# A four-head matrix-memory mixer: the attention moved into the o projection, memories handled in strips of 32, new states a projection later, stores from ScalarE's queue

## The reference

```python
w_inter = jnp.exp(inter - m_t)
s = jnp.einsum('bhtk,bhsk->bhts', q, k) * jnp.exp(d - m_t[..., None])
num = w_inter[..., None] * jnp.einsum('bhtk,bhkv->bhtv', q, C) + jnp.einsum('bhts,bhsv->bhtv', s, v)
den = w_inter * jnp.einsum('bhtk,bhk->bht', q, n) + jnp.sum(s, axis=-1)
h = num / jnp.maximum(jnp.abs(den), jnp.exp(-m_t))[..., None]
...
wk = w_k[..., None] * k
C_new = decay_prev[..., None, None] * C + jnp.einsum('bhsk,bhsv->bhkv', wk, v)
n_new = decay_prev[..., None] * n + jnp.sum(wk, axis=2)
```

## Time and profile before

| | |
|---|---|
| three runs | 2731.1 us median (2729.4 to 2731.57) |
| the profiled execution | span 2730.8 us from first to last instruction |
| TensorE, its weight loads | 2631.1 us (96%), 2523.8 us (92%) |
| VectorE, ScalarE, GpSimd | 1405.0 us (51%), 1004.8 us (37%), 222.7 us (8%) |
| heads | first projection from 47.28 us, the first gated layer from 713.77 us |
| mean granted clock of TensorE | 0.985 |
| HBM | 363.40 MB read, 23.43 MB written |

### The profile page before, as it was taken

One profiled execution on the slowest core, in us unless ns is written; L12 is line 12 of the kernel. 1 busy time (PEld: TensorE's weight loads), 2 busy tenths in 40 slices (PEclk: granted clock), 3 DMA queues, 4 the chain that ended last, 5 costly groups with the idle time before them and its releaser, 6 DMA issues. The chain is left out here.

```text
span 2730.8 us, 44822 instructions
## 1 busy us (share of the span) xinstructions
PE 2631.1 (96%) x16761; PEld 2523.8 (92%) x16761; DVE 1405.0 (51%) x2094; ACT 1004.8 (37%) x1345; POOL 222.7 (8%) x306
## 2 busy tenths in 40 slices
PE   7999999999999999999999997599999999999998
PEld 5969789797999999999999997599999999999997
DVE  5444444444754454454445446965455454554545
ACT  4323333233443332333333336244343342333435
POOL 1110201102200000000000003610000000000002
PEclk9999999999999999999999998799999999999999
DMA  4545445454344444444444434144444444444443
GB/s 137 163 153 164 164 124 166 156 163 162 125 143 149 144 140 141 140 140 133 151 144 133 147 128 134 48 142 149 153 144 151 149 147 149 146 149 148 141 141 108
DMA packets 224748, 389.77 MB, mean 143 GB/s; under 512 B 25829, under 2 KB 53045, under 8 KB 223965
## 3 DMA queue, kind: packets, MB, share of 16 engines
q1 hardware_dynamic: 222511, 382.93, 44.0%
q10 hardware_dynamic: 2045, 4.00, 0.4%
HBM read 363.40 MB, written 23.43 MB: 142 GB/s over the span
## 5 line engine op out<-in xcount | busy, mean ns | idle before, releaser
L1019 DVE TENSOR_TENSOR w_lo<-w_raw,w_hi 128x1024 fp32r<-128x1024 f32 x664 | 815.9, 1235 | 1043.8 <-ACT w_hi L759 1041.5
L759 ACT ACTIVATE w_hi<-w_raw 128x1024 fp32r<-128x1024 f32 x664 | 699.0, 1058 | 1364.6 <-PE bank L419 1328.8
L417 PE MATMUL bank<-xh,w_hi 128*128 128x336 f32 (+2 forms) x3584 | 1135.6, 317 | 49.6 <-issue 23.2
L418 PE MATMUL bank<-xl,w_hi 128*128 128x336 f32 (+2 forms) x3584 | 1129.7, 315 | 0.0
L419 PE MATMUL bank<-xh,w_lo 128*128 128x336 f32 (+2 forms) x3584 | 1127.4, 315 | 0.0
L417 PEld LDWEIGHTS bank<-xh,w_hi 128*128 128x128 f32 x3584 | 676.7, 189 | 58.5 <-issue 44.9
L419 PEld LDWEIGHTS bank<-xh,w_lo 128*128 128x128 f32 x3584 | 678.5, 189 | 0.0
L418 PEld LDWEIGHTS bank<-xl,w_hi 128*128 128x128 f32 x3584 | 677.7, 189 | 0.3
L417 PE MATMUL bank<-hh,w_hi 128*128 128x336 f32 (+1 forms) x1632 | 511.7, 314 | 4.5 <-issue 4.5
L419 PE MATMUL bank<-hh,w_lo 128*128 128x336 f32 (+1 forms) x1632 | 511.4, 313 | 0.0
L418 PE MATMUL bank<-hl,w_hi 128*128 128x336 f32 (+1 forms) x1632 | 511.3, 313 | 0.0
(11 more groups left out here) (247 smaller groups left out, 1257.4 us busy)
## 6 DMA issues: line engine op xcount, KB each, us to landing
w_raw<-in_w_up SPq DMA_DIRECT2D x640, 256.0 KB, 2.8
w_raw<-in_w_down SPq DMA_DIRECT2D x336, 256.0 KB, 3.4
w_raw<-in_w_mlstm_in SPq DMA_DIRECT2D x192, 256.0 KB, 3.1
area<-in_state_mlstm_C SPq DMA_DIRECT2D x32, 512.0 KB, 5.3
w_raw<-in_w_mlstm_out SPq DMA_DIRECT2D x64, 256.0 KB, 3.0
out_C_sample<-area SPq DMA_DIRECT2D x32, 512.0 KB, 3.0
w_raw<-in_w_up SPq DMA_DIRECT2D x64, 192.0 KB, 2.5
w_raw<-in_w_pool SPq DMA_DIRECT2D x16, 256.0 KB, 3.1
```

Source lines behind the costliest of these rows:

```text
L417: pe.matmul(out, wh, xhk, start=first, stop=False)
L418: pe.matmul(out, wh, xlk, start=False, stop=False)
L759: nc.scalar.activation(w_hi[:, s], w_raw[:, s], ACT.Copy).then_inc(hi_done, 1)
L1019: V.tensor_tensor(w_lo[:, s], w_raw[:, s], w_hi[:, s].bitcast(F32), ALU.subtract).then_inc(lo_done, 1)
```

## The change

What a head computes stays the same. The 64 sample tokens are padded: 8 sequences stand as 4 strips of 32 columns, each with 16 columns of padding and two sequences. All eight memories have a buffer, some of them in places that other tiles of the head use at another time; memory 0 shares its place with q and k.

- The o projection uses banks SA, so SB is free beside it. The transposed values stand before chunk 17, denominators and own numerators before chunk 19, past numerators before chunk 20, the transposes of the normalised heads before chunk 23. The prompt states stand behind chunk 23 and wait for banks of o that have been read out.
- Past numerators: 16 matmuls with 32 stationary columns, each group of four to four strips of one bank. New states: one fp32 matmul a memory and half of the keys, with 32 contracted rows (one strip holds two sequences; the weights of the other one are zero), in four rounds of four strips to four banks. These rounds, and VectorE's updates, stand in the q and k projection of the next head, and after the last head in the first projection of the first feed-forward. Stabilisers move from chunk 5 to chunk 7 in heads 1 to 3.
- Stores of new memories leave SP's queue for ScalarE's, four behind the high part of chunk 8 and four behind that of chunk 10. Loads of memories stand on SP before chunks 14, 16 and 18.
- Sums of squares and roots take places in the shared area in place of tiles of their own; GpSimd clears what is padded, and the split of keys and values for the new states is gone.

```diff
+TA = 3 * 128
+STRIPS, PER = 4, 2
...
+            def c_loads(h, batch):
+                for b in batch:
+                    if b == 0:
+                        wait_apart(sp, sp_passed, kt_ready, h + 1)
+                        wait_apart(sp, sp_passed, qm_ready, h + 1)
+                    elif not isinstance(h, int):
+                        sp.wait_ge(c_stored[b], 16 * h)
...
+                        if (blk, k) == (0, 6):
+                            if isinstance(h, int):
+                                sp.wait_ge(gcol_mm, 1)
+                            c_loads(h, (2, 4, 6))
+                        if (blk, k) == (1, 0):
+                            c_loads(h, (1, 3, 5, 7))
+                        if (blk, k) == (1, 2):
+                            c_loads(h, (0,))
...
-                    sp.wait_ge(c_updated, NB * h + b + 1)
-                    sp.dma_start(dst[b].rearrange("h (k p) v -> p (h k) v", p=P)[:, bass.ds(2 * h, 2), :],
-                                 Cr[:, b % 4]).then_inc(c_stored[b % 4], 16)
...
+            def new_states(h, e):
+
+                def products(r):
+                    i, k = r // 2, r % 2
+                    if r == 0:
+                        pe.wait_ge(evac, e)
+                        pe.wait_ge(wkb_ready, h + 1)
+                    else:
+                        pe.wait_ge(c_updated, 16 * h + 4 * r)
+                    for s in range(STRIPS):
+                        own = slice(32 * s, 32 * s + 32)
+                        pe.matmul(SB[s][:, :], wkb[own, i, k * P:(k + 1) * P], vtok[own, 2, :],
+                                  start=True, stop=True).then_inc(cnew_ready, 1)
+
+                return {at: (lambda r=r: products(r)) for r, at in enumerate((1, 2, 4, 5))}
...
+                def past_numerators():
+
+                    for b in range(NB):
+                        pe.wait_ge(c_landed[b], 16 * (h + 1))
+                    for i in range(PER):
+                        for k in range(2):
+                            for s in range(STRIPS):
+                                b = PER * s + i
+                                pe.matmul(SB[2][32 * s:32 * s + 32, :], qm[:, k, b, :], Cr[b][:, k, :],
+                                          start=False, stop=False, skip_group_check=True)
+                    pe.matmul(SB[2][:, :], PS2, vtok[:, 2, :], start=False, stop=True).then_inc(num_ready, 1)
...
-                gemm(SB, c, 16, KT, 4, xh, xl, 0, free=after(e + 4), amid={3: values})
...
-                    for k in range(2):
-                        new, ks = SB[2 * (b % 2) + k][:, :], slice(k * P, (k + 1) * P)
-                        pe.matmul(new, wkbh[0:TL, b % 2, ks], vh[0:TL, :], start=True, stop=False)
-                        pe.matmul(new, wkbh[0:TL, b % 2, ks], vl[0:TL, :], start=False, stop=False)
-                        m_ = pe.matmul(new, wkbl[0:TL, b % 2, ks], vh[0:TL, :], start=False, stop=True)
-                    m_.then_inc(cnew_ready, 1)
...
+                gemm(SA, c, 16, KT, 4, xh, xl, 0,
+                     guard={0: (ps_ready, h + 1), 1: (ktok_ready, h + 1)},
+                     amid={1: values, 3: own_numerators, 4: past_numerators, 7: hidden})
...
+                    pe.wait_ge(evac, e + (8 + (1, 4)[k]))
+                    for s in range(3):
+                        m_ = pe.matmul(SA[2 + k][:, :], wkp[:, s, k * P:(k + 1) * P], vtok[:, s, :],
                                        start=(s == 0), stop=(s == 2))
...
+            def c_stores(h, i):
+                for b in range(i, NB, PER):
+                    act.wait_ge(c_updated, 16 * h + 8 * (i + 1))
+                    act.dma_start(O["C_sample"][0][b].rearrange("h (k p) v -> p (h k) v", p=P)[:, bass.ds(2 * h, 2), :],
+                                 Cr[b]).then_inc(c_stored[b], 16)
...
                 his(c, 4, 9)
+                if not first:
+                    c_stores(h - 1, 0)
+                    his(c, 9, 11)
+                    c_stores(h - 1, 1)
...
+                if not first:
+                    dve.wait_ge(c_stored[0], 16 * h)
...
-                new_states(0, NB - 1)
...
+            def update(h, c, k0):
+
+                for r in range(4):
+                    i, k = r // 2, r % 2
+                    for s in range(STRIPS):
+                        b = PER * s + i
+                        dve.wait_ge(cnew_ready, 16 * h + (4 * r + s + 1))
+                        V.scalar_tensor_tensor(Cr[b][:, k], Cr[b][:, k], WI[:, NS * b + NS - 1:NS * b + NS],
+                                               SB[s][:, :], ALU.mult, ALU.add).then_inc(c_updated, 1)
+                    los(c, k0 + (4, 5, 7, 8)[r], k0 + (5, 7, 8, 9)[r])
...
+                    if first and q == 0 and i == 0:
+                        update(H - 1, c, k0)
+                        dve.wait_ge(c_stored[0], 16 * H)
+                        V.memset(E[:, :, 0:2], 0.0).then_inc(e_zero, 1)
+                        los(c, k0 + 9, k0 + 11)
...
+                for i in range(PER):
+                    m_ = G.tensor_scalar(wkb[:, i], ktok[:, 2], wsum[:, 4 + i:5 + i], None, ALU.mult)
+                m_.then_inc(wkb_ready, 1)
```

More of the change, by code:

```diff
@@ L181, in program, with owned @@
+        qn = view(15270, 2 * P).rearrange("p (k n) -> p k n", k=2)
+        Cr = [view(at, 2 * DV).rearrange("p (k n) -> p k n", k=2)
+              for at in [0] + [8614 + i * 2 * DV for i in range(6)] + [15526]]
+        def owned(ap, n=32):
+            return ap.rearrange("p (s c) -> p s c", c=n)[:, :, n - 16:]
         xtok = view(0, 3 * D).rearrange("p (s n) -> p s n", n=D)
@@ L184, in program @@
         ntok = view(6784, DK, NB * H)
[L185 to L188, removed]
+        wgr = view(8614, KT * 8).rearrange("p (k n) -> p k n", n=8)
+        wgg = view(8742, KT * 36).rearrange("p (k n) -> p k n", n=36)
+        sqr = view(9318, 4 * T).rearrange("p (s n) -> p s n", n=T)
+        row = [view(10662 + i * T, T, 36) for i in range(12)]
+        rpad = [view(7528 + i * P, P, H) for i in range(2)]
         E = view(0, 4 * GW).rearrange("p (f t) -> p f t", t=GW)
@@ L483, in sum_squares @@
                 pe.wait_ge(ssq_ready, k)
-                pe.matmul(out, ones[:, :], acc[:, :], start=True, stop=True).then_inc(rms_mm, 1)
+                pe.matmul(out, ones[:, :], sums[k], start=True, stop=True).then_inc(rms_mm, 1)
+            def new_states(h, e):
[11 more added lines that the diff above has]
+                return {at: (lambda r=r: products(r)) for r, at in enumerate((1, 2, 4, 5))}
             def head(h, c, e):
@@ new lines, in hidden @@
+                def hidden():
+                    pe.wait_ge(n_read, h + 1)
+                    pe.wait_ge(hn_ready, 3 * h + 3)
+                    for s, (t0, n) in enumerate(((0, P), (P, P), (2 * P, P))):
+                        for f in range(4):
+                            m_ = pe.transpose(SB[f][:, t0:t0 + n], hn[:, s, f * P:(f + 1) * P], ident[:, :])
+                    m_.then_inc(ht_ready, 1)
+                gemm(SB, c, 8, KT, 4, xh, xl, 0, free=None if first else after(e - 4), guard=guard, amid={2: scores})
@@ L597, in head @@
-                pe.wait_ge(den_read, h + 1)
-                for k in range(2):
-                    out = SA[3][:, 16 * k:16 * k + 1 + NB]
-                    pe.matmul(out, ktok[0:TL, 2, k * P:(k + 1) * P], X[0:TL, X2 + META - 1:XW:NS], start=True, stop=False)
-                    pe.matmul(out[:, 0:1], ktok[:, 0, k * P:(k + 1) * P], X[:, X1 - 1:X1], start=False, stop=False)
-                    m_ = pe.matmul(out[:, 0:1], ktok[:, 1, k * P:(k + 1) * P], X[:, X2 - 1:X2], start=False, stop=True)
@@ L1433, in _ @@
             sum_of_squares(1)
[L1435 to L1436 removed]
+            for b in range(NB):
+                pool.wait_ge(c_stored[b], H * 16)
             pool.wait_ge(cst_stored, 16 * H)
```

454 lines of the change are left out of this document (226 added, 228 removed).

## The result

The changed kernel takes 2658.0 us (median of four runs, 2656.3 to 2658.8) against 2731.2: 0.9731 of the time before, 95% interval 0.9717 to 0.9745. That is 73.2 us less. Predicted were 33 us less (2698); the measured time lies near the lower end of the stated range and beside the rival of four strips abreast (2654).

What follows compares the result with a forecast made beforehand. TensorE, busy 2631.1 of 2730.8 us, was taken as the bound. A head gains 27.5 + 0.6 − 17.8 − 1.4 − 0.2 − 0.7 = 8.0 us; four heads 32, with the start 33: 2698 us, own range 2685 to 2712, whole range up to 2734.

Steps and rivals of the forecast that it cites:

- four strips abreast: Rival for past numerators and new states: all four strips run together, 6.9 us a head, 2654 us; chance 0.14.
- The strips: Past numerators and new states: 32 strip matmuls at one pass each, with group ends and weight loads 17.8 us a head.
- loads of weights: New states: loading weights 128 columns wide shows once strips share the array, 16 × 0.11 = 1.8 us a head.
- The bound below: Lower bound for strip matmuls: four abreast, eight groups at 0.86 us, 6.9 us a head.
- One after another: Rival: strips do not overlap, 27.5 us a head; 2737 us, or 2749 if strip changes cost too; chance 0.17.
- a late queue: Rival: a store or wait on ScalarE, SP or VectorE holds something back four times; 2718 us, chance 0.11.
- The loop: Attention's loop over the eight memories, up to the prompt state, goes: 27.5 us a head gained.
- the prompt state waits: End of the o projection: new wait until a bank of o is read out, 0.7 us a head.
- the steps into and out of a round: Seven more pieces inside projections each cost 0.2 us beyond their work, 1.4 us a head.
- the start: Kernel start: VectorE no longer waits 2.24 us for GpSimd's clearing ahead of the gates; 1 us taken as gain.
- The forecast's own lower end: Lower end of the forecast's own range, 2685 us: loads of weights hidden, 1.8 us a head.
- What was costed at nothing: Updates, squares, normaliser and scaling beside projections, and the stores' and loads' queues: delays covered, no cost taken.

Runs made afterwards that it cites:

- The run with one strip: Changed kernel without the past numerators of strips 1 to 3 (12 of 16 matmuls a head left out): 2676.5 us, ratio 0.9800.
- the two orders: Changed kernel with past numerators reordered: four matmuls in a row on each strip, 2680.1 us; two in a row on each strip, 2659.0 us.
- the full rows: Changed kernel with new states contracting all 128 rows instead of a strip of 32: 2692.8 us, ratio 0.9857.
- the run on SyncE's queue: Changed kernel with the stores of updated memories put back from ScalarE's queue to SyncE's: 2657.3 us, ratio 0.9730.
- The mends: Changed kernel, first gated layer's rounds a chunk later: 2656.4 us; rounds before chunks 2, 4, 5, 6 and third bank of o read earlier: 2651.0 us.

## Why the prediction was wrong

The direction and what bounds the kernel were right; the size was off by 40.0 us (2698 − 2658.0), and one step of the sum failed.

*The strips.* The step was that "the next strip's first pass starts no earlier than that second pass", so that a strip matmul costs 0.43 us: 17.8 us a head. The first passes of four strips start together, and their second passes too. The steps measured are 3.57 + 4 × 1.07 = 7.85 us a head; 9.95 less, over four heads 39.8 of the 40.0. The run with one strip shows that the other three cost nothing, the two orders show how far ahead a strip starts, and the full rows price the other half. The 1.8 us for loads of weights was too much: four rounds take 4 × 0.21 = 0.8 us a head more than the 0.86 of one matmul each, and no run shows how much of that is loads.

That one step makes 39.8 of the 40.0 is in part luck. The denominators below (1.6 us over four heads) and the first round at the gated layer (3.4) went the other way. The stretch behind that layer's first sum of squares, which holds none of the moved work, took 1981.3 us in the profiled execution after and 1986.9 before (from 674.34 and 743.89 us to the ends); over the other versions, but for the one with the stops, it is 1980.9 to 1985.3. Where these few microseconds come from was not shown.

*The rivals.* Four abreast (2654) was the case, at a chance of 0.14. What spoke against it, "the order of the passes", was an argument from fp32 matmuls that all used the same cells; no row of before could carry it to strips. The bound below, 6.9 us a head, was near the 7.85 measured. The Trainium skill, "TensorE: Matmul & The Clock Gate", Part 3, has a gain of 3.07 for four row strips, by which the text had 2663, nearer than my sum. The traces roughly agree: 3.43 / 1.07 = 3.2 for the rounds, and 27.5 / 7.85 = 3.5 for all. One after another fell with the same rows, and so did a late queue: no store and no landed memory stands on TensorE's list of waits, and the run on SyncE's queue takes the same time.

*The other terms* were mostly of the right size. The loop was 27.5 on the mean; the prompt state waits 0.60 (0.7); the steps into and out of a round still cost 0.2 (the step before L502 is 0.24, the one behind L422 0.26, against 0.15), though the full rows show that not every piece in a projection pays it; the start came 0.85 us earlier (1), and behind GpSimd's clearing VectorE indeed waits for something else, a load. The forecast's own lower end did not follow from its term: 1.8 us a head gives 2691, not 2685. The denominators were missed: padded to 128 columns they take 1.70 us a head instead of 1.30.

*What was costed at nothing* holds inside the heads but for the 0.46 us ahead of the second head's first round: updates, stores and loads are hidden there although issues and landings are slower than in the earlier trace rows. It fails behind them: "the stretch behind the heads keeps its length" missed that the last head's rounds wait for banks which VectorE reads late there, 1.76 us, with half clock behind it. The mends show that it could be had back. It hid in the total, since the strips gave so much more.

## What to carry to other kernels

In this kernel small fp32 matmuls on different 32-wide strips of rows or columns run four abreast, in both passes. Put them in turn over the strips, where the block costs what its longest strip costs; two in a row cost no more, four in a row cost 5.2 us more a block, and three were not run. Part of the gain of making TensorE's work short is lost where the other engines' chain behind it has no cover, so place such pieces inside a long projection. And when a price lies between two bounds far apart, a mechanism thought up for it, which no row shows, is no evidence for a value between them.

## What the runs showed of the hardware that was not expected

- Leaving work out can cost time: 12 fewer matmuls a head made the kernel 18.5 us slower, through three stops of 2.7 to 3.35 us at the starts of iterations of a later loop and half clock behind each. With the same number of instructions the stops were gone, and none of the other versions has them. That they come from fetching the loop's code was not shown. The Trainium skill, "Runtime: NRT & Kernel Launch", Instruction fetch mechanics, has code fetched in blocks and a taken branch stall where its target is not at hand. That would fit in part; the stops stand one matmul behind the start of an iteration.
- Fp32 matmuls on different strips overtake each other: strip 1 began ahead of strip 0's fourth matmul, and short matmuls on strips 1 to 3 ahead of strip 0's second.
- A round in row strips costs 0.41 us beyond its passes, the same round on all rows nothing.
- Idle times of 1.76 and 4.0 us were each followed by 1.2 GHz. In another execution (stores on SyncE's queue) the same 1.76 us were not: the clock is 1.00 behind them, and there the second round waited 1.63 us for VectorE instead. The second round of the changed kernel, then both rounds of that execution:

```profile
647.87 1.14 PE L502 MATMUL bank<-area 32*128 32x512 f32 x8
...
641.67 1.14 PE L512 MATMUL bank<-area 32*128 32x512 f32 x8 [1.76 <-DVE x L1063]
648.37 1.14 PE L512 MATMUL bank<-area 32*128 32x512 f32 x8 [1.63 <-DVE area L1251]
```

The two rounds begin 6.7 us apart in either execution (641.17 to 647.87, 641.67 to 648.37): where VectorE sets the pace, the lower clock cost nothing of its own.
